# Second tokens' attention in pairs of units inside the expert loop: both exponents of a pair in one ScalarE step

## What is computed

```python
h = rms_norm(x, norm1_g) * (1.0 + sc1) + sh1
x = x + g1 * token_mixer(h, ...)          # NSA (compressed, selected, window) and DSA heads
h = rms_norm(x, norm2_g) * (1.0 + sc2) + sh2
x = x + g2 * peer_ffn(h, ...)             # 8 heads, top 16 of 128 x 128 experts each
...
ue = u[ec]; ve = v[ec]                    # 128 experts per token, rows of 1024 floats
act = gelu(einsum("cd,chkd->chk", xc, ue))
out = einsum("chk,chkd->cd", gc * act, ve)
```

## Time and profile before

| | us |
|---|---|
| median of 3 runs | 974.0 |
| lowest and highest | 964.36 and 974.45 |
| the profiled execution | 961.43 |
| its span, first to last instruction | 959.6 |
| first gather issued | 256.49 |

### The profile page before, as it was taken

One profiled execution on the slowest core, in us unless ns is written; L12 is line 12 of the kernel. 1 busy time (PEld: TensorE's weight loads), 2 busy tenths in 40 slices (PEclk: granted clock), 3 DMA queues, 4 the chain that ended last, 5 costly groups with the idle time before them and its releaser, 6 DMA issues.

```text
span 959.6 us, 9707 instructions
## 1 busy us (share of the span) xinstructions
PE 790.7 (82%) x2908; PEld 435.9 (45%) x2908; DVE 649.6 (68%) x1674; ACT 411.1 (43%) x1150; POOL 288.2 (30%) x260
## 2 busy tenths in 40 slices
PE   3999899999878987888876888786887777777775
PEld 2544678889834543455553554332322222222221
DVE  5532559984577869785848676877867668576644
ACT  3211312351368687542324544545534344343433
POOL 0000000000233454634433535434354342533420
PEclk8899999999978999999999999999899999999999
DMA  9975227771299999999999999999999999999992
GB/s 371 421 320 218 88 88 287 291 311 76 98 368 372 401 389 422 402 419 419 420 417 420 420 419 420 422 420 421 422 421 421 421 423 421 420 422 421 420 423 113
DMA packets 47476, 342.84 MB, mean 357 GB/s; under 512 B 5377, under 2 KB 6593, under 8 KB 10689
## 3 DMA queue, kind: packets, MB, share of 16 engines
q0 software_dynamic: 36864, 268.45, 67.8%
q1 hardware_dynamic: 10112, 73.31, 19.1%
q10 hardware_dynamic: 448, 0.46, 0.2%
HBM read 341.16 MB, written 1.05 MB: 357 GB/s over the span
## 4 chain that ended last, share of the span: by engine, by line
DMA 42%; PE 33%; DVE 11%; ACT 6%; issue 4%; POOL 3%; another core or an unknown queue 0%; DVEq 0%; SPq 0%; POOLq 0%; ACTq 0%
DMA extra<-in_uv,arena 21%; DMA ring<-in_uv,arena 11%; DMA arena<-in_uv,arena 9%; PE banks L751 8%; PE banks L521 5%; PE banks L487 4%; PE banks L473 3%; PE banks L704 2%; DVE extra L1591 2%; PE banks L723 2%; PE banks L693 2%; POOL arena L854 1%; DVE arena L1591 1%; PE banks L627 1%; ACT L1078 1%
## 5 line engine op out<-in xcount | busy, mean ns | idle before, releaser
L751 PE MATMUL banks<-extra 128*128 128x512 f32 x500 | 248.7, 630 | 62.1 <-ACT extra L1088 58.9
L854 POOL DMA_INDIRECT extra<-in_uv,arena x136 | 154.8, 1138 | 444.5 <-DVE arena L1574 293.8
L1078 ACT ACTIVATE arena<-arena 128x1 f32<-128x1 f32 x256 | 51.6, 202 | 325.2 <-DVE arena L1591 310.9
L751 PEld LDWEIGHTS banks<-extra 128*128 128x128 f32 x500 | 90.1, 195 | 198.6 <-ACT extra L1088 108.2
L751 PE MATMUL banks<-arena,extra 128*128 128x512 f32 x296 | 143.5, 612 | 35.2 <-ACT extra L1088 33.7
L1591 DVE CUSTOM_DVE_ANT_0 extra<-extra 128x1024 f32<-128x1024 f32 x80 | 97.7, 1225 | 52.2 <-DMA extra<-in_uv,arena 51.3
L854 POOL DMA_INDIRECT arena<-in_uv,arena x80 | 88.9, 1111 | 123.7 <-PE banks L751 51.8
L751 PEld LDWEIGHTS banks<-arena,extra 128*128 128x128 f32 x296 | 51.4, 190 | 118.8 <-ACT extra L1088 71.3
L1088 ACT ACTIVATE extra<-tab,arena 128x128 f32<-128x128 f32 x235 | 94.3, 401 | 7.7
L1591 DVE CUSTOM_DVE_ANT_0 extra<-extra,arena 128x1024 f32<-128x1024 f32 x56 | 68.7, 1227 | 41.8 <-DMA extra<-in_uv,arena 37.3
L751 PE MATMUL banks<-ring,extra 128*128 128x512 f32 x144 | 73.8, 639 | 26.9 <-ACT extra L1088 26.3
(11 more groups left out here) (253 smaller groups left out, 1056.6 us busy)
## 6 DMA issues: line engine op xcount, KB each, us to landing
arena<-in_w_late SPq DMA_DIRECT2D x24, 512.0 KB
arena<-in_w_ada SPq DMA_DIRECT2D x5, 2048.0 KB, 8.6
arena<-in_w_in SPq DMA_DIRECT2D x4, 2048.0 KB, 21.3
extra<-in_w_gate SPq DMA_DIRECT2D x3, 2048.0 KB, 8.9
extra<-in_w_ada SPq DMA_DIRECT2D x3, 2048.0 KB, 8.6
arena<-in_w_ada SPq DMA_DIRECT2D x4, 1024.0 KB, 11.4
extra<-in_w_ada SPq DMA_DIRECT2D x4, 1024.0 KB, 27.8
extra<-in_w_br SPq DMA_DIRECT2D x2, 2048.0 KB, 14.8
```

The lines of the kernel that those rows point to most:

```text
L751: last = nc.tensor.matmul(acc[tt][:, half * 512:(half + 1) * 512], diag[i % DIAGS], uv_slot[SLOT[v]][:, D + half * 512:D + (half + 1) * 51 ...
L854: nc.gpsimd.indirect_dma_start(uv_slot[SLOT[g]], None, A["uv"], bass.IndirectOffsetOnAxis(ap=expert[:, g:g + 1], axis=0)).then_inc(uv_in[S ...
L1078: link(nc.scalar.activation(gel[:, v:v + 1], dots[:, v:v + 1], ACT.Gelu))
```

## The change

The 12 units are placed in pairs. PAIR_AT gives the step a of each pair: 2, 8, 14, 20, 26, 32. Both units' scores are made on TensorE in step a. From then on the first unit counts as placed at a and the second at a + 1: masks on VectorE in a + 3 and a + 4 (`unit_mask` still stands at BEHIND = 3 after the unit's step), both units' exponents on ScalarE in step a + 5, one after the other; transposes in a + 7 and a + 8, copies and outputs in a + 10 and a + 11, and `finish` six steps (2 x BEHIND) after the transposes, which makes steps 22, 34 and 46, as before. All AT_ constants behind the attention are 3 higher. MORE goes from 56 to 63 and MOST from 119 to 126, so 7 slots are used for 7 steps longer, and 9 slots for as many steps as before.

```diff
--- before.py
+++ after.py
@@ -152,7 +152,7 @@
 
 
 
-MORE, MOST = 56, 119
+MORE, MOST = 63, 126
 SLOT = [g % 7 if g < MORE else (7, 8, 0, 1, 2, 3, 4, 5, 6)[(g - MORE) % 9] if g < MOST else
         (9, 10, 7, 8, 0, 1, 2, 3, 4, 5, 6)[(g - MOST) % 11] for g in range(STEPS)]
 USE = [SLOT[:g].count(SLOT[g]) for g in range(STEPS)]
@@ -165,9 +165,11 @@
 PE_NO = {v: i for i, v in enumerate(ON_PE)}
 DVE_NO = {v: i for i, v in enumerate(ON_DVE)}
 
-UNIT_AT = {2 + 3 * i: EACH + i for i in range(EACH)}
-AT_OT, AT_BR, AT_OUT, AT_SSQ, AT_WQ, AT_H2ROW = 47, 51, 69, 88, 94, 113
-AT_BLK, AT_X1ROW, AT_G2ROW, AT_OUT0 = 1, 117, 128, 143
+PAIR_AT = {2 + 6 * i: (EACH + 2 * i, EACH + 2 * i + 1) for i in range(EACH // 2)}
+UNIT_AT = {a + i: u for a, pair in PAIR_AT.items() for i, u in enumerate(pair)}
+EXP_AFTER, TURN_AFTER = 5, 7
+AT_OT, AT_BR, AT_OUT, AT_SSQ, AT_WQ, AT_H2ROW = 50, 54, 72, 91, 97, 116
+AT_BLK, AT_X1ROW, AT_G2ROW, AT_OUT0 = 1, 120, 131, 146
 
 
 BEHIND = 3
@@ -789,14 +791,14 @@
             pe.wait_ge(sub_ready, HEADS)
 
             for g in range(STEPS + 1):
-                if g in UNIT_AT:
-                    unit_scores(UNIT_AT[g])
+                for u in PAIR_AT.get(g, ()):
+                    unit_scores(u)
                 if g - 1 in PE_NO:
                     value_step(g - 1)
-                if g - BEHIND - 2 in UNIT_AT:
-                    unit_transposes(UNIT_AT[g - BEHIND - 2])
-                if g - 2 * BEHIND - 2 in UNIT_AT:
-                    unit_output(UNIT_AT[g - 2 * BEHIND - 2])
+                if g - TURN_AFTER in UNIT_AT:
+                    unit_transposes(UNIT_AT[g - TURN_AFTER])
+                if g - TURN_AFTER - BEHIND in UNIT_AT:
+                    unit_output(UNIT_AT[g - TURN_AFTER - BEHIND])
                 if g == AT_BLK:
                     block_scores(1)
                 if g == AT_BLK + 2 * BEHIND:
@@ -1094,10 +1096,10 @@
             for g in range(STEPS):
                 b, i = divmod(g, BLOCK)
                 diagonal(g)
-                if g - BEHIND in UNIT_AT:
-                    unit_exp(UNIT_AT[g - BEHIND])
-                if g - 2 * BEHIND - 2 in UNIT_AT:
-                    unit_pt(UNIT_AT[g - 2 * BEHIND - 2])
+                for u in PAIR_AT.get(g - EXP_AFTER, ()):
+                    unit_exp(u)
+                if g - TURN_AFTER - BEHIND in UNIT_AT:
+                    unit_pt(UNIT_AT[g - TURN_AFTER - BEHIND])
                 if i == 8 and b + 1 < BLOCKS:
                     gate_exponent(b + 1)
                 if g == AT_BLK + BEHIND:
@@ -1650,9 +1652,9 @@
                         expert_sums(b + 1, 0, BLOCK)
                     if i == 11:
                         normalize(b + 1)
-                if g - 3 * BEHIND - 2 in UNIT_AT and UNIT_AT[g - 3 * BEHIND - 2] % 4 == 3:
-                    finish(UNIT_AT[g - 3 * BEHIND - 2] // 4)
-                    if UNIT_AT[g - 3 * BEHIND - 2] == len(UNITS) - 1:
+                if g - 2 * BEHIND - TURN_AFTER in UNIT_AT and UNIT_AT[g - 2 * BEHIND - TURN_AFTER] % 4 == 3:
+                    finish(UNIT_AT[g - 2 * BEHIND - TURN_AFTER] // 4)
+                    if UNIT_AT[g - 2 * BEHIND - TURN_AFTER] == len(UNITS) - 1:
                         heads_done(1)
                 if AT_BR <= g - 2 - BEHIND < AT_BR + 2 * KT and (g - 2 - BEHIND - AT_BR) % 4 == 0:
                     merge(1, (g - 2 - BEHIND - AT_BR) // 4)
```

## The result

The changed kernel takes 998.1 us in the median of 4 runs (987.98 to 999.35), the kernel before 972.4 (964.36 to 974.45). The ratio is 1.026, with a 95% interval of 1.017 to 1.035. It is slower by 25.7 us; the interval leaves out 1, but not a loss under 2%. I had predicted 969 us with a range up to 979, and gave a loss of over 1% one chance in ten: the prediction was wrong.

The account below looks back on a forecast made before the run. From about 395 us gathers at 421 GB/s set the pace; only 10.0 us of lost DMA time before could move. Terms -4.1 + 1.6 = -2.5 us gave 969 us, between 966.7 and 971.5; range 957 to 979.

Parts of the forecast that it names:

- What bounds the kernel, and the accounting of lost rate: Gathers at 421 GB/s set the pace from about 395 us; only 10.0 us lost from 275 to 395 could return.
- Table loads: ScalarE: ten of 31 table loads go, freeing 12.8 us, mostly into its idle time.
- the 4.1 us of gaps: Lost-rate stretches at 350 to 360, 300 to 320 and 385 to 395 us give back 1.5, 2.0 and 0.6.
- rival 2: No change: what ScalarE gives back, the first pair's scores take; 961.4 and 974.0 us; chance 0.18.
- Both scores in step a: TensorE: the second unit's scores delay a slot's release, unhidden only at the first pair, step 2; costs 1.6 us.
- Seven slots longer: GpSimd's gathers 56 to 62 wait for the step seven before; cost 0, bound 5.0 us.
- A longer hold on ScalarE: Diagonal to diagonal takes 5.8 us six times instead of 4.68 twelve times; cost 0, upper bound 6.7 us.
- Rival 3, the falling clock: TensorE's clock falls behind each pair: +9.2 us, 970.6 by the profile, 983 by the median; chance 0.13.
- five windows of 5 us with a clock below 0.8: Sign for the rival of TensorE's falling clock: five or more such windows between 285 and 395 us.
- the drain that the prediction weighed and left out: ScalarE: a skill page adds about 1380 ns per table switch, 26.6 us freed instead of 12.8; not used.

Follow-up runs that it names:

- e5: Changed kernel with ScalarE's copy ahead of the pair's exponents and four masked-score buffers instead of two; 701.3 us from first gather to end, ratio 1.006.
- e8: Kernel before with four buffers for the masked scores instead of two; 700.6 us from first gather to end, ratio 1.000.
- e4: Kernel before with only the late half: MORE and MOST at 63 and 126, AT_ constants three higher; 704.1 us from first gather to end, ratio 0.997.
- e3: Changed kernel with the second unit's scores one step later, at a + 1; 727.4 us from first gather to end, ratio 1.030.
- e9: Kernel before with transposes, copies, outputs and finish two steps later, plus MORE, MOST and AT_ constants as changed; 707.5 us from first gather, ratio 1.005.
- e10: Kernel before with four score buffers, each copy behind another unit's exponents, and MORE, MOST and AT_ constants as changed; 701.8 us from first gather, ratio 0.999.
- e1: Changed kernel with ScalarE's copy of the transposed scores ahead of the pair's exponents; 712.1 us from first gather to end, ratio 1.007.
- e2: Changed kernel with four buffers for the masked scores instead of two; 713.6 us from first gather to end, ratio 1.011.
- e11: Changed kernel with a pair's two exponents in separate ScalarE steps, a + 4 and a + 5; 728.1 us from first gather to end, ratio 1.030.
- e6: Changed kernel with 16 needless TensorE matmuls ahead of each pair's second output; 727.8 us from first gather to end, ratio 1.020.

## Why the prediction was wrong

**What bounds the kernel, and the accounting of lost rate: right.** 10.0 us lost before, 36.1 after, and the difference is the loss. From 437 us on the rate is 421, as said. At most 10 us were there to gain, and no version gained anything that can be told from nothing.

**Table loads: right in size, without value.** Ten loads, 12.5 us of ScalarE's busy time for 12.8 predicted. e5 keeps the joint exponents and removes the stalls; it stands at 701.3 us against 703.1 of the kernel before and e8's 700.6, which both have all the loads. So of the 4.1 us of gaps that were to close thanks to the loads nothing is seen that exceeds the differences between single profiles. That was rival 2, "no change", for this term; what holds those gaps open was not traced.

**Both scores in step a: about right at the first pair.** The two gathers in question in the changed kernel:

```profile
268.13 1.53 POOL L856 DMA_INDIRECT extra<-in_uv,arena  x1 [267.68 <-DVE arena L1576]
...
294.05 1.39 POOL L856 DMA_INDIRECT extra<-in_uv,arena  x1 [9.56 <-PE banks L753]
```

294.05 - 268.13 = 25.9 us against 280.14 - 256.49 = 23.7 before: 2.3 us later, where I had 1.6. In part this is luck, for the clock of the first steps differs between executions: the first two scores took 3.76 us here and 2.47 in e5, which has them in the same place and issues this gather at 22.0 us. e3, with the second scores a step later, has it at 24.0.

**Seven slots longer: right**, nothing (e4).

**"A longer hold on ScalarE": this is the step that failed, twice.** First, I named as queued behind the pair's exponents "the Gelu, the product and the diagonal of step a + 6". The copy of the pair before is queued there too: the second unit's copy stands at a + 11, the exponents of the next pair at a + 6 + 5 = a + 11, the same step, and the text puts the exponents first. Before, exponents stood at s + 3 and copies at s + 8, with units every three steps; 3 and 8 never meet. The term on gaps has the same error in words: the wait for the copy "stays tied to `diagonal` of its own step as before". It doesn't; for the second unit it is now tied to a pair's exponents. The hold was put at 0, with 6.7 us as its bound. Second, the mask's waits are no term of the prediction at all: they were put at nothing without a reason. The mask waits for TensorE's scores, but also for the transposes of two units earlier, since scores have two buffers. Before, that is s + 3 against (s - 6) + 5 = s - 1: four steps. Now it is a + 3 against (a - 6) + 7 = a + 1: two. The transposes moved two steps later, the mask didn't move, and VectorE lost half of its lead. I wrote the new steps down in the section on the change and didn't subtract them. What the two made is a wait of 32.6 us for the mask and 10.0 more for the outputs, and 26.1 us in all.

**Rival 3, the falling clock: its sign came, and I had given it 0.13.** I had asked for five windows of 5 us with a clock below 0.8 between 285 and 395 us. The changed kernel has ten (from 285, 290, 320, 325, 340, 345, 350, 370, 375 and 390 us), eight if the two at the start of its loop are left out; the kernel before has three. Its price of +9.2 us was too small. What I held against it, that the outputs at a + 4 and a + 5 give TensorE work while it waits, fails by the first error: the output at a + 5 is the operation that stands waiting for the copy. The low clock goes away with the two couplings (e5: three windows, as before), so it comes with the stalls; how much of the loss it carries is not settled, and the rows above put it at up to 13 us.

**Why it is 26 us and not 4.** Each coupling alone, put into the kernel before, costs 3.4 us (the mask's, e9) or nothing that can be told (the copy's, e10). With pairs each alone costs 9.0 and 10.5 us (e1, e2), and both together 26.1, more than their sum. My reading of the chain is that the lateness of one round is handed to the next: ScalarE's copy waits behind exponents that wait for nothing but the loop, TensorE's scores and value steps wait behind the output of that copy, VectorE's mask and all dots behind it wait for the transposes, ScalarE's next copy and exponents wait for the dots. Seven slots cover a stall that is over when the next one begins; they don't cover a ring that takes 22.2 us for six steps. That the ring closes is read from the chain and from e1, e2 and e5; how the 26 us divide among the scores, the length of the hold and the clock once it is closed was not separated. The scores' place (1.8 us, e3) and the joint exponents (1.1, e11) change little alone; for the clock e6 gives only a net with its filler.

**The range** ended at 979 because the bounds were made of prices of single stalls: 6.7 us for the hold, 9.2 for rival 3. The hold's upper bound assumed that a hold delays only what stands directly behind it. A bound on an edit that shortens the distance between two engines should be that of the loop running at the pace of the ring: at 22.2 us for six steps instead of 14.9, five pairs lose 5 x 7.3 = 37 us (an estimate from the round above, seen only after the run).

## What to carry to other kernels

When operations of a hand-made pipeline are moved, write for each semaphore wait the step of the waiter minus the step of the one waited for, before and after, also for the waits that only guard a buffer; and for each engine the list of what shares a step modulo the new period, in program order. A distance that shrinks is the first suspect, before any busy time. If a buffer is two deep and work now comes in twos, it is one deep.

## What the runs showed of the hardware that was not expected

**Much of the spread between executions lies before the loop.** The code ahead of the first gather is the same in all these kernels, yet the profiles have the first gather between 256.5 and 268.6 us. Two windows of the kernel before:

```profile
100.00:150.00 50.00, 45.66 (x279) 37.63 (x278) 32.00 (x96) 14.46 (x48) 0.00 (x0) 0.97 0.32 112
...
200.00:257.00 57.00, 52.23 (x422) 49.30 (x422) 32.11 (x107) 19.32 (x45) 0.51 (x1) 0.97 0.37 154
```

and of the changed kernel:

```profile
100.00:150.00 50.00, 45.66 (x261) 37.37 (x260) 28.57 (x89) 13.21 (x43) 0.00 (x0) 0.90 0.26 90
...
200.00:257.00 57.00, 52.23 (x360) 47.92 (x358) 28.76 (x74) 18.02 (x43) 0.00 (x0) 0.85 0.39 158
```

TensorE's mean granted clock is 0.97 and 0.97 in the one and 0.90 and 0.85 in the other: at 1.2 GHz for part of the time in one execution and hardly in the other, in a stretch where the order and the work are equal. The 12 us are as much as the spread of the timed runs of the kernel before (964 to 974), and the six kernels without a loss, which differ by 12.1 us up to the first gather, differ by only 3.5 us from there on. What makes the one execution keep its clock was not tried, and that the clock makes the whole 12 us is read from these windows, not tested. It means that whole spans of single profiles can't be compared here; the first gather has to be subtracted.

**No idle time stands round a table load.** In all 13 profiles every load from 260 to 520 us starts 0.01 to 0.03 us after the ScalarE instruction before it ends, and the next instruction can start 1.29 us after the load's start; the drain that the prediction weighed and left out shows in none. In the changed kernel it is 317.65 - 316.35 = 1.30 us from the load's start to the exponent's, as in the earlier trace rows.
